# Differential attention taken in pairs of heads inside a two-layer trunk kernel

## The reference

```
q, k = rms(q_raw), rms(k_raw)            # 4 heads, 2 maps each, 64 wide; v is 128 wide
for each block of 128 queries:
    s  = q @ k.T * scale - slope[head] * |distance|, causal
    p  = softmax(s)                      # one map for m = 0, one for m = 1
    a  = p[m=0] - lam * p[m=1]
    o  = a @ v
o = rms(o) * (1 - lambda_init)
y_conv = B * conv3(C * v_conv)           # 512 channels, 3 taps
x += W_out(sum of gate_i * (branch_i @ W_i));  x += PEER(rms(x));  x += gated per-layer input
```

## Time and profile before

| | |
|---|---|
| runs shown | 3731.59, 3730.33, 3715.93 us; median 3730.33 |
| the profiled execution | 3718.08 us, span 3716.2 us |
| busy, share of the span | PE 78%, DVE 67%, ACT 38%, POOL 36% |
| mean granted TensorE clock | 0.891 |
| DMA | 1298.54 MB, 349 GB/s over the span |

### The profile page before, as it was taken

One profiled execution on the slowest core, in us unless ns is written; L12 is line 12 of the kernel. 1 busy time (PEld: TensorE's weight loads), 2 busy tenths in 40 slices (PEclk: granted clock), 3 DMA queues, 4 the chain that ended last, 5 costly groups with the idle time before them and its releaser, 6 DMA issues.

```text
span 3716.2 us, 28796 instructions
## 1 busy us (share of the span) xinstructions
PE 2911.9 (78%) x8144; PEld 1481.8 (40%) x8144; DVE 2492.2 (67%) x5163; ACT 1427.6 (38%) x3952; POOL 1328.1 (36%) x1033
## 2 busy tenths in 40 slices
PE   7699848868989788777988788868999775555556
PEld 4454614535436334433446234525436331111112
DVE  1311486877667877867658877777667977777773
ACT  2230224457433344456432344457433342222222
POOL 0000033334332343344333443334332445555551
PEclk9789979989999899989999899889999997777778
DMA  4214379989998999989998999999998999999994
GB/s 153 82 68 154 106 320 378 390 328 404 407 390 343 395 408 389 395 339 422 418 384 329 409 409 374 357 361 391 418 389 344 398 408 420 422 421 422 421 422 185
DMA packets 182400, 1298.54 MB, mean 349 GB/s; under 512 B 20320, under 2 KB 21856, under 8 KB 26592
## 3 DMA queue, kind: packets, MB, share of 16 engines
q0 software_dynamic: 147456, 1073.81, 71.1%
q1 hardware_dynamic: 34784, 222.88, 15.2%
HBM read 1294.51 MB, written 2.10 MB: 349 GB/s over the span
## 4 chain that ended last, share of the span: by engine, by line
PE 47%; DMA 22%; DVE 15%; ACT 11%; issue 5%; POOL 1%; SPq 0%; DVEq 0%; ACTq 0%; POOLq 0%
DMA ring<-in_uv,experts 18%; PE ps_sum L1318 12%; PE ps_act L1380 8%; PE ps_act L1552 8%; PE ps_act L1425 7%; DVE ring L1192 5%; DMA wt<-in_weights 4%; PE ps_dve L1380 3%; DVE x L1201 2%; PE ps_dve L1580 2%; ACT diag L775 1%; ACT weight L769 1%; ACT area_e L554 1%; PE ps_dve L1425 1%; ACT L554 1%
## 5 line engine op out<-in xcount | busy, mean ns | idle before, releaser
L524 POOL DMA_INDIRECT ring<-in_uv,experts x1024 | 1325.6, 1295 | 2318.1 <-DVE x L1201 886.7
L1318 PE MATMUL ps_sum<-ring,diag 128*128 128x512 f32 x2120 | 1218.7, 719 | 625.0 <-ACT diag L775 620.7
L1192 DVE SCALAR_TENSOR_TENSOR ring<-ring,h_ffn 128x1024 f32<-128x1024 f32 x1024 | 1234.8, 1220 | 232.4 <-DMA ring<-in_uv,experts 225.8
L1318 PEld LDWEIGHTS ps_sum<-ring,diag 128*128 128x128 f32 x2120 | 437.7, 220 | 1297.7 <-ACT diag L775 895.4
L1201 DVE SCALAR_TENSOR_TENSOR x<-ring,weight,x 128x1024 f32<-128x1024 f32 x494 | 633.3, 1282 | 204.2 <-ACT weight L769 204.2
L767 ACT ACTIVATE dots<-dots 128x1 f32<-128x1 f32 x1024 | 205.3, 201 | 1376.8 <-DVE ring L1192 1374.5
L1425 PE MATMUL ps_act<-area_h,wt 128*128 128x256 f32 x1536 | 345.2, 383 | 2.4 <-ACT area_h L540 2.4
L1552 PE MATMUL ps_act<-wt,area_h 128*128 128x512 f32 x768 | 339.0, 596 | 5.6 <-DMA wt<-in_weights 5.6
L1380 PE MATMUL ps_act<-wt,area_h 128*128 128x512 f32 (+1 forms) x768 | 332.5, 593 | 5.5 <-ACT area_h L540 5.3
L1425 PEld LDWEIGHTS ps_act<-area_h,wt 128*128 128x128 f32 x1536 | 293.2, 192 | 58.2 <-issue 15.3
L769 ACT ACTIVATE weight<-dots,gate 128x1 f32<-128x1 f32 x1024 | 301.6, 295 | 33.3
(11 more groups left out here) (171 smaller groups left out, 2048.2 us busy)
## 6 DMA issues: line engine op xcount, KB each, us to landing
wt<-in_weights SPq DMA_DIRECT2D x192, 1024.0 KB, 8.9
ring<-in_uv,experts POOLq DMA_INDIRECT x1024, 12.5
wt<-in_weights SPq DMA_DIRECT2D x12, 512.0 KB, 9.0
wt<-in_weights SPq DMA_DIRECT2D x4, 768.0 KB, 8.9
x<-in_x SPq DMA_DIRECT2D x4, 512.0 KB, 5.1
area_y<-in_keys SPq DMA_DIRECT2D x4, 512.0 KB, 9.9
area_f<-in_keys SPq DMA_DIRECT2D x4, 512.0 KB, 11.1
area_f<-in_ffn_rows SPq DMA_DIRECT2D x4, 512.0 KB, 4.0
```

What stands on the lines that cost most here:

```text
L524: pool.indirect_dma_start(ring[:, row.slot, :], None, a[f"uv{row.step // 2}"][:, :], bass.IndirectOffsetOnAxis(ap=experts[:, row.step % 2, ...
L1192: dve.scalar_tensor_tensor(u, u, 1.0, h_ffn[:, row.tile, :], ALU.mult, ALU.mult, accum_out=dots[:, row.j:row.j + 1]).then_inc(dots_ready, 1)
L1318: ins = pe.matmul(ps_sum[:, b, :], diag[:, row.pe_before % DIAGS, :], ring[:, row.slot, D + b * 512:D + (b + 1) * 512], start=row.pe_first ...
```

## The change

```diff
-def attention(kind, d, heads, between):
-    out, n, between = [], 2 * heads, list(between)
-    for i in range(n + 3):
-        if i < n:
-            out.append((kind + "_scores", d, i))
-        if i >= 1 and between:
-            out.append(between.pop(0))
-        if 2 <= i < n + 2:
-            out.append((kind + "_flip", d, i - 2))
-        if i >= 3:
-            out.append((kind + "_pv", d, i - 3))
-    return out + between
+def diff_by_pairs(d):
+    between = {0: [("conv_c", d, 0)], 2: [("conv_c", d, 1), ("conv_x", d, 0)], 4: [("conv_x", d, 1), ("conv_b", d, 0)],
+               6: [("conv_b", d, 1), ("taps", d)], 8: [("latent", d)], 10: []}
+    out, n = [], 2 * DH
+    for i in range(0, n + 4, 2):
+        more = list(between[i])
+        out += [("diff_scores", d, i + k) for k in range(2) if i < n]
+        out += more[:1]
+        out += [("diff_pv", d, i - 4 + k) for k in range(2) if 0 <= i - 4]
+        out += more[1:]
+        out += [("diff_flip", d, i - 2 + k) for k in range(2) if 0 <= i - 2 < n]
+    return out
...
 def rows_in(stage):
-    if stage[0] == "mla_scores":
-        return 0 if stage[2] % 2 else 2 * ROWS_IN["mla_scores"]
+    if stage[0] in ("mla_scores", "diff_scores"):
+        return 0 if stage[2] % 2 else 2 * ROWS_IN[stage[0]]
     return ROWS_IN[stage[0]]
...
-        out += attention("diff", d, DH, [("conv_c", d, 0), ("conv_c", d, 1), ("conv_x", d, 0), ("conv_x", d, 1),
-                                         ("conv_b", d, 0), ("conv_b", d, 1), ("taps", d), ("latent", d)])
+        out += diff_by_pairs(d)
...
-        diff_prob = [area_e[:, 0:1024], area_e[:, 1024:2048], area_b[:, 2048:3072]]
+        diff_prob = [area_e[:, 0:1024], area_e[:, 1024:2048], area_b[:, 2048:3072], area_b[:, 4096:5120]]
...
-                dve.wait_ge(evacs, WHERE[("diff_flip", d, i - 3)].evacs + 1 if i >= 3 else at.evacs)
+                dve.wait_ge(evacs, WHERE[("diff_flip", d, i - 4)].evacs + 1 if i >= 4 else at.evacs)
...
                 dve.wait_ge(act_ops, WHERE[("diff_scores", d, i)].act + 2)
-                op(dve.reciprocal(inv[:, i % 4, :], total[:, b, :]))
+                if i >= 4:
+                    dve.wait_ge(evacs, WHERE[("diff_pv", d, i - 4)].evacs + 1)
+                op(dve.reciprocal(inv[:, b, :], total[:, b, :]))
```

More of the change, by code:

```diff
@@ L631, in diff_scores @@
             def diff_scores(at, d, i):
-                b, w = i % 3, width_of(d, i // DH)
+                b, w = i % 4, width_of(d, i // DH)
                 act.wait_ge(taken, at.taken + 2)
@@ L909, in diff_scores @@
                 t, h = divmod(i, DH)
-                b, w = i % 3, (2 * (d % 2) + t + 1) * P
-                dve.wait_ge(evacs, WHERE[("diff_flip", d, i - 3)].evacs + 1 if i >= 3 else at.evacs)
+                b, w = i % 4, (2 * (d % 2) + t + 1) * P
+                dve.wait_ge(evacs, WHERE[("diff_flip", d, i - 4)].evacs + 1 if i >= 4 else at.evacs)
                 link()
@@ L918, in diff_flip @@
             def diff_flip(at, d, i):
-                b, w = i % 3, (2 * (d % 2) + i // DH + 1) * P
+                b, w = i % 4, (2 * (d % 2) + i // DH + 1) * P
                 dve.wait_ge(act_ops, WHERE[("diff_scores", d, i)].act + 2)
-                op(dve.reciprocal(inv[:, i % 4, :], total[:, b, :]))
+                if i >= 4:
+                    dve.wait_ge(evacs, WHERE[("diff_pv", d, i - 4)].evacs + 1)
+                op(dve.reciprocal(inv[:, b, :], total[:, b, :]))
                 link()
                 p0, p1 = diff_prob[b][:, 0, 0:w], diff_prob[b][:, 1, 0:w]
-                op(dve.scalar_tensor_tensor(inv_lam[:, b, 0:1], inv[:, i % 4, 1:2], lam[:, d // 2, 3:4], total[:, b, 0:1],
+                op(dve.scalar_tensor_tensor(inv_lam[:, b, 0:1], inv[:, b, 1:2], lam[:, d // 2, 3:4], total[:, b, 0:1],
                                             ALU.mult, ALU.mult))
@@ L1483, in diff_flip @@
                 pe.wait_ge(dve_ops, at.dve + 3)
-                flip(diff_prob[i % 3][:, 0, :], 2 * (d % 2) + i // DH + 1)
+                flip(diff_prob[i % 4][:, 0, :], 2 * (d % 2) + i // DH + 1)
             def diff_pv(at, d, i):
```

## The result

In 20 executions of each kernel on one chip the changed kernel took 3733.72 us (3725.27 to 3744.32) and the kernel before 3726.24 us (3715.93 to 3733.85). The ratio is 1.0023, with an interval of 1.0013 to 1.0033: slower by 7.5 us where a gain of about 9 was forecast. The number lies in the range, and in the case "within 0.5%", but on the other side of zero. The profiled execution took 3725.27 us with a span of 3723.4, so 7.2 us more than the profiled execution before.

A forecast was written before the change was run, and what follows sets the result against it. Pass 0 was taken as bound by its own chain, passes 1 to 3 by engines coupled in order under a 418 GB/s ceiling. Terms -6.5 + 0.5 + 0 - 3 = -9 us gave 3709 or 3721 by basis; forecast 3717, range 3693 to 3737.

The forecast's parts named there:

- within 0.5%: Case that the whole kernel's time changes too little to tell from no change (about 18.6 us); chance 0.65.
- Passes 1 to 3: Attention passes beside rows: same 34 rows per pass, two more on PE in pass 1; +0.5, 0 and -3 us.
- Pass 1, +0.5: Pass 1 walked in the new order: latent starts 1.5 us later, pv 7 ends 0.5 us later.
- Up to scores 2: Pass 1: PE row between scores 2 and 3 waits 2.3 us, the 2.2 us wait before flip 0 disappears; even.
- Taps: Pass 1: VectorE reaches taps no earlier; PE waits some 1.5 us more there than the 3.12 and 2.71 before.
- Passes 2 and 3, 0 and -3: Pass 2 unchanged; pass 3 gains 3 us, part of 7.9 us more VectorE waiting for scores than in pass 1.
- Pass 0, -6.5: Pass 0: shorter flip waits (5.5 and 1.2) less 0.6 and 0.9 save 5.2 us, plus 1.3 us from the clock.
- The clock term: Latent in pass 0 runs at a higher clock after a shorter PE gap: 1.3 us saved, between 0 and 2.
- Pairs help beside rows too: First rival: PE's flip waits vanish in passes 1 to 3, -24 us, with pass 0 -30; 3688 to 3701; chance 0.26.
- The second, a PE row between two scores: Rival: second scores of pairs wait behind a PE row, +36 us less 6.5; 3748 to 3761; chance 0.08.
- Only pass 0 counts, and the rest takes it back: Third rival: +1.5 at taps in each pass, no gain in pass 3; about 0, 3718 to 3730; chance 0.2.
- Small parts: Table loads (18 fewer, 23 us of ACT, hidden), weight tiles, the added wait and the 4th buffer: counted as nothing.

The follow-up runs named there:

- the two rows were turned alone: Pairs in all passes with the split of before, only rows 45 and 53 moved to PE; pass 1's segment 118.4 us against 111.6.
- rows 48 and 64 alone: Pairs in all passes with the split of before, only rows 48 and 64 moved to VectorE; pass 1's segment 115.1 us against 111.6.
- the order alone: Changed kernel (pairs in all passes), but each row on the same engine as in the kernel before: 3705.29 us, ratio 0.9952 against before.
- the 149 later rows: Pairs everywhere, split of before in step 0, new split from step 1 on: 3721.37 us, ratio 1.0001 against before.
- the fourth set: Four kernels: pairs with old split again (3705.84 us), pass 0 in old order (3708.44), row 61 on PE (3706.66), a mixture (3707.79); before 3724.53.
- The kernel of row 61: Pairs with the split of before, but row 61 on PE and the new split from diff_sub of pass 2 on in step 1; one execution, 3698.35 us.
- the mixture: Pairs in passes 0 and 1 (old split, row 61 on PE), single heads with new split inside passes 2 and 3: 3707.79 us, ratio 0.9962.
- the best one: Pairs in all passes with the split of the kernel before, measured twice: 3705.29 us (0.9952) and 3705.84 us (0.995).
- the six rows: Pairs everywhere, new split only in step 0 (rows 45, 48, 53, 61, 64, 67 change engine): 3721.96 us, 0.9993; the changed kernel has them too.

## Why the prediction was wrong

**The step that failed** is in "Passes 1 to 3": "two more go to PE in pass 1 ... and +3 rows in the whole kernel, 5.7 us of PE beside 3.6 less of DVE." It took a count for the effect. The count is right (530 to 533); but 155 rows change engines, and that enters no term of the sum and none of the rivals. By the runs it is worth -5 us in the old order and +27 to +34 in the new one (from 0.995 to 1.0023 and 1.0041), so it outweighs the 16 to 19 us that the order gains, and the kernel came out slower. I walked the rows with the new engines at each stage of pass 1, so their positions were in the walk, but only there, and with two errors.

**Pass 1, +0.5.** Measured +5.8 (125.4 against 119.6). The two errors of the walk:
- "Up to scores 2 ... PE, which adds it between scores 2 and 3 and waits some 2.3 us for its diagonal ... Even." The code hands rows of the even scores on, and adds them after the *odd* ones, and PE waits there for a bank instead (2.51 us), whoever adds the row. So the row is not a wait exchanged for a wait but 1.8 to 3.1 us laid bare; the same at scores 4. "Even" twice was +3.6 in the changed kernel, and +6.8 where the two rows were turned alone.
- "Taps: ... now I get some 1.5 us more." The direction was right; rows 48 and 64 alone cost 3.5, and from the convolution after scores 7 to latent the changed kernel loses 5.0.
- Not in the walk at all: rows at the lower clock, above all the one of 3.78 us between flips 0 and 1, and the two of 5.17 us after scores 7.

**Passes 2 and 3, 0 and -3.** Pass 2's segment went from 112.7 to 112.3 us, pass 3's from 123.2 to 117.8 (121.5 in the second profiled execution), about as said or better. In the order alone they are 111.1 and 116.7, and pass 1 is 111.6: -1.6, -6.5, -8.0. So the order gains 16 us in passes 1 to 3, where my own forecast had 2.5.

**What lies outside the passes** had no term at all, and most of what the 149 later rows cost (0.49%) sits there: in their own trace the segments of passes 2 and 3 are only 1.8 and 1.0 us longer than in the order alone. From `diff_sub` of pass 2 to the first `mla_scores` it is 93.5 to 95.4 us with the new split against 86.9 to 88.1, in either order. A part of it comes back up to `ffn_norm` (499.1 to 503.7 us against 502.4 to 506.9). From pass 3's first `mla_scores` to its `ffn_norm` it is 503.3 to 507.1 against 496.9 to 500.1. No sentence of the prediction looked there.

**Pass 0, -6.5.** In the trace it came out as worked. The PE timeline of the changed kernel at flip 0, flips 4 and 5, latent and the last pv:

```profile
93.39 0.33 PE L1469 MATMUL ps_act<-ident,area_e 128*128 128x128 f32 x1 [1.23 <-DVE area_e L929]
...
122.91 0.44 PE L1469 MATMUL ps_act<-ident,area_e 128*128 128x128 f32 x2 [2.28 <-DVE area_e L929]
...
124.04 11.34 PE L1381 MATMUL ps_act<-wt,area_h 128*128 128x416 f32 x32
...
137.15 1.13 PE L1478 MATMUL ps_act<-kept_diff_v,area_f 128*128 128x128 f32 x8 [0.31 <-ACT area_f L539]
```

2.28 us where 7.85 was the earlier trace rows, for 2.3 worked out (2.28 or 2.29 in all 13 traces that have pairs in pass 0); PE's waits for flips fall from 10.3 to 3.9 us, those for banks rise from 0.3 to 1.1 (I had +0.9); latent took 11.34 for 13.10; the last pv ends at 138.3 where 140 was named and 146 was. The segment goes from 78.1 to 70.0 us. But at the end of the kernel it is hardly there: pairs in pass 0 alone make the kernel 1.1 us faster, with an interval that holds zero; and with against without it in the fourth set, 3705.84 against 3708.44, gives 2.6. One execution's pass 0 is not another's: with the same instructions the segment is 70.0 us in two traces and up to 76.3 in others (the old order has 75.9 to 78.4), and from its start to `ffn_norm` of pass 0 it is 414.8 us in two traces, 418.0 in one and 420.7 to 422.0 in ten, where the old order has 423.4 to 425.0 in five. The profiled execution was at the lucky end, with a granted clock of 0.82 from 196 to 246 us where before had 0.69 and the second profiled execution of the changed kernel 0.70. The clock term (1.3 us) is the one that varies: latent took 11.34 us in five of the 13 traces, 12.35 to 12.45 in seven and 13.03 in one. The mechanism was right; the size at the end is 1 to 3 us and not 6.5.

**The rivals.** Nearest to what the order does is the first, "Pairs help beside rows too": PE's waits for flips do go (8.0 us in pass 1, 0.4 with pairs and the split of before) and what replaces them is smaller. Its size was -24 to -30; the order alone gives -16 to -19. The second, a PE row between two scores, never arises, since the code puts it behind the pair; its relative did, at a price of 1.8 to 3.1 us a place instead of 4.06. (Its own bar of 8.4 us per pass asks for more than two places at 4.06.) The third ("Only pass 0 counts, and the rest takes it back") names the outcome, and its reason is half right: the rows at the taps cost more, but so did those at scores 2, 4 and 6. Its sum takes 3 x 2 us where the walk had 1.5.

**Small parts.** The 18 table loads are hidden as said: they go in all kernels with pairs in passes 1 to 3, the slow one too, with ACT busy some 50 of the 112 to 125 us of pass 1's segment. Weight tiles and the added wait: nothing, by the kernel with old order and four buffers (1.0004).

**Left open.** Why the shifted pattern of the later split costs some 6 us ahead of `mla_scores` of pass 2 and again at the end of pass 3. PE's waits for diagonals in the first of the two, in the old order, are these, for the kernel before and with the new split:

```profile
PE ps_sum L1318 <- ACT diag L775: 16.5, 4, 6.1
```
```profile
PE ps_sum L1352 <- ACT diag L807: 21.6, 4, 9.7
```

PE waits 5 us longer, once for 9.7 us. The kernel of row 61 narrows it down: of the 57 rows of that step it has the 46 from `diff_sub` of pass 2 on turned, and the stretch is 92.6 us, as was expected of it; with only the rows inside passes 2 and 3 turned (the mixture) it is 87.6. So it is the rows of that stretch and not those of the pass. But in that trace all of it was back at `ffn_norm` (500.6 us against 506.9), and the execution was at the fast end of all that ran, 3698.35 us, so what these rows cost at the end is open. Why the changed kernel lost 7.5 us on one chip and 17 on another, while both measurements of the best one agree within 3 us, is open too (with intervals that overlap, it may be chance); pass 0 and pass 3 differ between its two profiled executions, and pass 1 does not (125.4 in both).

## What to carry to other kernels

Where a plan derives the share of each engine from the order of the stages, a new order is two changes: compare the derived lists entry by entry, not their totals, and measure new order with old split and old order with new split, since here each gained (16 to 19 us, and 5) and both together lost 7 to 17. Before giving an engine one more piece of work, look at what stands right before it: behind a standstill it was paid in full here, in some traces at a lower clock. And read such a case in segments cut at instructions, which here mostly repeat within 2 us in passes 1 to 3 (pass 3 of the changed kernel once did not, 117.8 and 121.5), rather than in the total alone, whose executions differ by up to 20 us.

## What the runs showed of the hardware

The spread that was not expected is pass 0's. There no DMA of rows runs, the same order of work took 70.0 to 76.3 us by execution at granted clocks of 1.00 to 0.91, and one and the same kernel 70.0 and 72.9, another 76.1 and 72.9. The granted clock of 196 to 246 us is 0.69 to 0.83. The Trainium skill, page "TensorE: Matmul & The Clock Gate", section "Why this matters for your kernels", asks that PE has no long gaps; the shorter gap (2.28 for 7.85 us) went with latent at 11.34 us in five of the 13 traces, as that rule has it, and latent took 12.57 to 13.35 us behind 7.85 us in all five traces of the old order. But it took 12.35 to 13.03 us in the other eight, behind the same 2.28 us. And 0.70 and 0.82 for the same kernel between 196 and 246 us show that the same order of work can come to either level. In pass 1 the clock went with the waits: 0.95 to 0.97 with pairs and the split of before, 0.91 or 0.92 in the four traces with the six rows as well. A single place is not decided by them: behind the same standstill of 2.51 us the same row took 2.88 us in one trace and 1.98 in four, and the convolution that follows at once where there is no row took 7.17 us at a granted clock of 1.00 in pairs with the split of before, and 8.86 us with rows 48 and 64 turned.
